# Three edits to a two-layer diffusion step: the wait ahead of GpSimd's LayerNorm pass, the place of four attention loads, and the order of the first transposes

## The reference

```python
m = silu(cvec) @ ada_w + ada_b                  # (1024) x (1024, 6144), per layer
# layer 0: proj = h @ w_in_a -> q, k, v, p;  differential attention over [cache_k | k], [cache_v | v],
#          centred pooling of p;  out = concat(a, pooled) @ w_out_a;  then a dense SwiGLU
q, k, v, p = split(h @ w_in_a);  k_all = concat([cache_k, rope(k)])
x = LN(alpha * x + gate * out) * ln_g + ln_b
ff = (silu(h @ w_gate) * (h @ w_up)) @ w_down
# layer 1: gates and q, k, v, o = h @ w_in_c -> bidirectional mLSTM -> @ w_out_c;  top-2-of-8 expert SwiGLU
```

## Time and profile before

| | us |
|---|---|
| runs | 1464.95, 1465.63, 1466.57 |
| the profiled execution: time / span | 1464.95 / 1463.3 |
| PE busy | 1382.3 (94% of the span) |
| DVE busy | 886.1 (61%) |
| ACT busy | 725.0 (50%) |
| POOL busy | 212.0 (14%) |
| mean granted PE clock | 0.984 of full speed |

### The profile page before, as it was taken

The page is one execution under the profiler, slowest core; times in us unless marked ns, Lnnn a source line. Parts: engine busy times, 40 slices in busy tenths (PEclk is TensorE's granted clock), DMA queues, the critical chain, the costliest instruction groups (busy, mean ns, idle before and its releaser), DMA issues.

```text
span 1463.3 us, 20876 instructions
## 1 busy us (share of the span) xinstructions
PE 1382.3 (94%) x6966; PEld 1139.1 (78%) x6966; DVE 886.1 (61%) x1182; ACT 725.0 (50%) x1120; POOL 212.0 (14%) x278
## 2 busy tenths in 40 slices
PE   6989889999999989998979899999999999999997
PEld 2766468999999979986657788888888888878884
DVE  0325557463333475323885597655555899999997
ACT  1323555332333353322444586444444888888883
POOL 1010000070000002203420453200000610000010
PEclk9999989999999999999999799999999999999999
DMA  9796654459444424437665599766655999999991
GB/s 346 221 308 214 202 194 128 145 181 370 120 128 130 139 64 130 131 125 254 208 214 194 171 381 373 256 186 204 216 187 181 336 382 377 384 374 380 378 361 58
DMA packets 255110, 341.23 MB, mean 233 GB/s; under 512 B 16910, under 2 KB 210732, under 8 KB 254908
## 3 DMA queue, kind: packets, MB, share of 16 engines
q1 hardware_dynamic: 241354, 299.55, 61.9%
q0 software_dynamic: 12400, 40.67, 7.4%
q10 hardware_dynamic: 1282, 0.04, 0.0%
HBM read 318.12 MB, written 21.02 MB: 232 GB/s over the span
## 4 chain that ended last, share of the span: by engine, by line
PE 83%; DVE 8%; ACT 3%; issue 3%; DMA 2%; SPq 0%; POOL 0%; DVEq 0%; ACTq 0%
PE PS L2212 25%; PE PS L504 14%; PE PS L2219 12%; PE PS L480 7%; PE PS L481 7%; PE PS L482 7%; PE PS L623 2%; PE PS L2187 1%; DMA raw<-in_w_in_a 1%; DMA BIG<-in_poolm 1%; ACT BIG L1555 1%; PE PS L648 1%; DMA raw<-in_ada_w 1%; PE PS L1799 1%; DVE Hl L2085 1%
## 5 line engine op out<-in xcount | busy, mean ns | idle before, releaser
L456 DVE TENSOR_TENSOR wlo<-raw,whi 128x1024 fp32r<-128x1024 f32 x130 | 168.1, 1317 | 230.9 <-ACT whi L453 230.8
L2017 DVE TENSOR_TENSOR wlo<-BIG,whi 128x1024 fp32r<-128x1024 f32 x192 | 239.3, 1262 | 68.8 <-ACT whi L2013 67.3
L2013 ACT ACTIVATE whi<-BIG 128x1024 fp32r<-128x1024 f32 x192 | 202.8, 1060 | 66.3 <-PE PS L2212 39.7
L2212 PE MATMUL PS<-whi,Hh 128*128 128x512 f32 x560 | 223.3, 399 | 2.3 <-DVE Hl L2085 2.2
L2212 PE MATMUL PS<-whi,Hl 128*128 128x512 f32 x560 | 219.3, 392 | 0.0
L2212 PE MATMUL PS<-wlo,Hh 128*128 128x512 f32 x560 | 219.1, 391 | 0.0
L480 PE MATMUL PS<-Hh,whi 128*128 128x384 f32 (+1 forms) x624 | 209.0, 335 | 4.8 <-DVE Hl L787 3.0
L481 PE MATMUL PS<-Hl,whi 128*128 128x384 f32 (+1 forms) x624 | 207.7, 333 | 0.0
L482 PE MATMUL PS<-Hh,wlo 128*128 128x384 f32 (+1 forms) x624 | 207.5, 333 | 0.0
L2017 DVE TENSOR_TENSOR wlo<-raw,whi 128x1024 fp32r<-128x1024 f32 x144 | 177.2, 1242 | 48.0 <-ACT whi L2013 46.6
L2013 ACT ACTIVATE whi<-raw 128x1024 fp32r<-128x1024 f32 x144 | 152.2, 1059 | 57.2 <-PE PS L2219 30.9
(11 more groups left out here) (388 smaller groups left out, 1960.9 us busy)
## 6 DMA issues: line engine op xcount, KB each, us to landing
raw<-in_moe_w_gu SPq DMA_DIRECT2D x224, 256.0 KB, 6.0
BIG<-in_moe_w_gu SPq DMA_DIRECT2D x224, 256.0 KB, 6.1
raw<-in_ada_w SPq DMA_DIRECT2D x96, 512.0 KB, 5.0
BIG<-in_moe_w_down SPq DMA_DIRECT2D x80, 512.0 KB, 7.7
raw<-in_ffn_w_gu SPq DMA_DIRECT2D x44, 512.0 KB, 4.9
raw<-in_w_in_c SPq DMA_DIRECT2D x32, 512.0 KB, 4.0
raw<-in_moe_w_down SPq DMA_DIRECT2D x32, 512.0 KB, 7.3
scr_tok<-BIG POOLq DMA_DIRECT2D x28, 512.0 KB, 9.9
```

Source lines behind the costliest of these rows:

```text
L456: self.eng.tensor_tensor(wlo[:, s, :], raw[:, s, :], whi[:, s, :].bitcast(f32), ALU.subtract).then_inc(lo_made, 1)
L2013: act.activation(whi[:, slot(v), :], moe_raw(v), ACT.Copy).then_inc(hi_made, 1)
L2017: dve.tensor_tensor(wlo[:, slot(v), :], moe_raw(v), whi[:, slot(v), :].bitcast(f32), ALU.subtract).then_inc(lo_made, 1)
L2212: last = pe.matmul(PS[:, 6 * b + c % 2, :], lhs, wt[:, s, 512 * k:512 * k + 512], start=(q == 0 and k == 0 and lhs is h and wt is whi), st ...
```

## The change

Three edits. First, POOL's in-place LayerNorm pass for the first two norms no longer waits for a count of used units (12 units into the FFN, and 8 units into the `w_in_c` stage) but for `hl_made`, which DVE raises when the split input of the next stage is complete: 6 after the first norm, 9 after the second. Second, the four attention loads on POOL's queue stand ahead of the three bias loads of the `MID` quantities and wait for unit 16 (t0) instead of unit 33. Third, at the start PE does all 24 transposes of x in one piece after four ada units, and the next eight ada units in one piece behind them.

```diff
@@ pool_norm
             for t in range(TT if st < 3 else TT - 1):
                 if st < 2:
-                    pool.wait_ge(unit_used, (U_FFN + 12, U_INC_T + 8)[st])
+                    pool.wait_ge(hl_made, TT * (st + 2))
@@ gpsimd
             pool_ada(pool, FIRST)
-            pool_ada(pool, MID)
-            pool.wait_ge(unit_used, U_INA_T + 18)
+            pool.wait_ge(unit_used, U_INA_T + 1)
             pool.dma_start(ck, ...).then_inc(att_loaded, 16)
             pool.dma_start(cv, ...).then_inc(att_loaded, 16)
             pool.dma_start(pw, ...).then_inc(att_loaded, 16)
             pool.dma_start(pm..., a["poolm"]).then_inc(att_loaded, 16)
+            pool_ada(pool, MID)
             pool.wait_ge(v_made, 1)
@@ tensor
             pe.wait_ge(lam_step, 5)
-            ada.units(2)
             pe.wait_ge(x_loaded, 48)
             for t in range(TT):
                 pe_turn(pe, 0, t)
-                ada.units(2)
+            ada.units(KT)
             pe.wait_ge(modc_read, 1)
```

## The result

The changed kernel takes 1484.88 us (median of four runs, 1483.31 to 1488.55), against 1466.10 of the kernel before in as many. The ratio is 1.0128, with a 95% interval of 1.0100 to 1.0154: **18.8 us slower**. The forecast was 1476.0, with a range up to 1480. The sign and the places were right, the size was not. The profiled execution took 1485.15 us (span 1483.5, mean granted clock 0.975), 20.2 more than the one of before.

The account below looks back on a forecast made before the run. PE, with 83% of what ended last, was taken to bound the kernel, so edits count by PE's waits. First pass 6.8, second 1.8, loads 2.4, transposes 0 gave +11.0 on 1464.95: 1475.95, said as 1476, range 1468.5 to 1480.

Parts of the forecast that it names:

- The LayerNorm pass, first time: At the FFN's start: POOL's earlier pass delays DVE and stalls PE ahead of u1; 6.8 us in all, 5.6 to 8.3.
- The turns: At the FFN's start: DVE's splits and POOL's operations alternate, so a split takes 3.42 us instead of 1.23.
- the lower case: Ahead of u1: DVE is in first, its first split takes 1.23 us, and PE stalls 4.4 us.
- The same pass, second time: At the start of w_in_c: late DVE work holds PE at the fourth unit; 1.8 us, 0.7 to 2.9, low end 0.
- A stall of this length has a second price: At u1: after 3.0 us without work PE runs at half clock for 2.8 us; 1.3 us lost, 1.2 to 1.7.
- The loads: At t3 and t4: attention loads moved beside t units delay them, less a saved 1.0 us wait; net +2.4 us, -1.0 to +3.8.
- the bound: At t3: PE first waits for all attention loads; unit 25 lands at 61.2, t3 is 4.2 us late, net +3.8.
- The two queues share about equally: Ahead of t3: unit and attention loads progress alike, unit 25 lands about 60.4, t3 starts 3.3 us late.
- turns packet by packet: In the loads ahead of t3: each DMA engine goes round-robin between its queues, so the edit costs +2.4 us.
- The transposes: At the start: 24 transposes fit into PE's idle time and unit 11 lands as before; 0 us, -0.9 to +1.0.
- The clock stays low beyond u1: Rival, from the FFN's u1 on: slow clock lasts longer, or zero writes meet a thin ring; +15 us, 1480, chance 0.08.

## Why the prediction was wrong

**The LayerNorm pass, first time: right in mechanism and size.** The turns are 3.3 us (3.42 forecast), five splits with DVE first take 14.53 (14.91 forecast), L1285 follows, and PE waits 3.8 for it. I took 5.5, the middle of 4.4 and 6.6; it was the lower case, and 0.6 under that, since each of the four turns was 0.1 shorter (0.4 together) and PE came to u1 12.9 us after L816 (270.62 - 3.80 - 253.94) instead of 12.7. The clock behind it cost 1.6 where 1.3 stood, in the 1.2 to 1.7. Together 5.4 (5.6 to 8.3 forecast); the run with this half alone says +5.6. In the traces of that run and of the one with both halves the slow stretch was twice as long, and the stage 6.5 to 6.6 us longer, so the clock cost up to 2.8.

**The same pass, second time: mechanism right, sum far short.** The wait of 2.7 lies at the upper end of 0.7 to 2.9. (That range is narrower than its own terms: two operations that lose 1 to 2.3 us each put L1488's end at 551.6 to 556.4, not at 552.4 to 554.6. Measured, they lost 0.9 and 2.1, behind splits with POOL in first.) But the step "A stall of this length has a second price" was applied to u1 only, with a stall of 5.5 in mind. The clock fell to its lower level behind this stall too (1.7), and once more behind the old gap of 1.6 at 661 us (1.7), which the pass alone does not explain. 6.1 where 1.8 stood; the run with this half alone says +6.8.

**The loads: the bound, not the share.** "The two queues share about equally" failed, and with it the +2.4 that the forecast drew from turns packet by packet: unit 25 landed behind the last of the attention loads, and t3 waited 4.8, not 3.3 and beyond the bound of 4.2. And again the clock: 2.4 us that had no term. The chain behind it came out as forecast: t4 and later units moved with t3, t6 waited 1.3 (1.4 before), L1017 no longer waits. +5.7 where +2.4 stood; the run with the loads alone says +5.7.

**The transposes: nothing, as forecast,** +0.9 with an interval that holds 0. The reason given was not quite right: unit 11 did land late, by 1.7 us and beyond the 1.0 allowed, as PE comes to units 4 and 5 only at 21.73, behind 4.91 us of transposes, and the units that take their slots are issued later. That it cost nothing in the changed kernel is due to the idle time ahead of t0 and, in its profiled execution, to where the slow stretch fell.

**The sum.** Forecast 6.8 + 1.8 + 2.4 = 11.0; in the profile 5.4 + 1.7 (526 us) + 6.1 + 6.1 + 1.0 (attention) = 20.3. All waiting of PE together was forecast almost exactly: 5.5 + 1.8 + 3.3 - 1.0 = 9.6, against 3.8 + 2.7 + 4.8 - 1.1 = 10.2. The missing 9 us are PE working at 1.2 GHz: 1.3 forecast, 10.1 in the profile. **The step that failed is the second price**, reckoned for one stall of three. Filling the three stalls gives 5.7 back in the timed runs and, between fixed points, 2.1 behind t3, 1.35 behind u1 and 3.1 in `w_in_c`, which shows that part. The rest (526 us, attention) is only read from the trace, and stands or is missing in other kernels whatever they change there. Why the clock falls behind such a gap in one execution and not in another no run settles. The ledger is also of one execution each, and that of before was a quick one: 20.2 us apart, where the medians are 18.8. Of the rivals, "The clock stays low beyond u1", at 0.08 and 1480, was the nearest.

## What to carry to other kernels

The new stalls of PE of 2.7 to 4.8 us cost here, besides themselves, 1.6 to 2.8 us of half clock each; behind those of 1.3, 1.5 and 2.4 us at t3 (`pm` or the small tiles early, `pm` early with fillers) the clock was 1.00. Price each stall so, not only the longest, and widen the range by one or two such stretches at gaps that the change does not touch. Work moved forward on an idle engine should wait for the step that the critical engine waits for, not for its own data: POOL's pass behind L1285 and L1488 is free, behind `hl_made` it costs 12 us. A stream of loads without slack took 6.8 us of others at a price both early and late, and the next unit landed behind all that was issued around it. And compare two kernels stage by stage, between fixed points, in more than one trace: a slow stretch in a single trace need not be the edit's.

## What the runs showed of the hardware

- GpSimd's memsets into SBUF, 128x1024 in 1.0 us each, leave VectorE's splits at 1.16 each (4.63 for four); its tensor_tensor makes them 3.37.
- A tensor_scalar of 16x384 from SBUF to SBUF is held too: L1487 took 1.21 beside POOL's pass and 0.35 in before. Operations that read PSUM kept their length (L1485 0.61, L1486 0.56, L1285 0.54).
- 24 transposes in one piece took 4.91 us (0.20 each), where before each eight between units took about 1.1 (0.14 each). No run takes this apart.
- Strict turns slow GpSimd as well: its operation beside a split took 3.2 to 3.5 instead of 2.4.
- The same gap of PE is not always followed by the same clock: 1.61 us ahead of L504 at 643 us in before, then 1.00; 1.61 at 661 us after, then 0.50 for 3.4 us.
- Nor are the same instructions always run at the same clock: six kernels with the same instructions up to the first norm reach the first attention output at 134.1 to 136.3 us, by where their slow stretches fall.
